# Retention over the prompt in chunks of 128, stacked sample rows in w_out, two expert slots loaded early, refills without a limit

## The chip, the cores and the metric

The kernel runs on one core of a Trainium2 chip, in one launch, in fp32 (some matmul operands are split into a high and a low part). The metric is the device time of one execution in microseconds. Engines: PE = TensorE, DVE = VectorE, ACT = ScalarE, POOL = GpSimd, SP = SyncE, which only issues DMAs here.

## What is computed

One inference step of one decoder layer for a prompt of 512 tokens and for 8 samples of 4 tokens each (32 rows), model width 1024. The token mixer has four retention heads (128 wide) and eight block-sparse attention heads (64 wide), a gated merge and an output projection; a layer norm, a mixture of 32 experts (two chosen per token within one of four groups) and a second layer norm follow. The retention of the prompt, as the reference has it:

```python
def retention_chunk(state, q, k, v):            # q, k, v of one chunk, L = 128
    log_g = jnp.log(retention_gammas())         # gamma_h = 1 - 2 ** (-5 - h)
    idx = jnp.arange(L, dtype=F32)
    diff = idx[:, None] - idx[None, :]
    decay = jnp.where(diff >= 0, jnp.exp(log_g[:, None, None] * jnp.maximum(diff, 0.0)), 0.0)
    inner = jnp.einsum('bhij,bhjv->bhiv', jnp.einsum('bhid,bhjd->bhij', q, k) * decay, v)
    q_dec = q * jnp.exp(log_g[:, None] * (idx + 1.0))[:, :, None]
    cross = jnp.einsum('bhid,bhdv->bhiv', q_dec, state)
    k_dec = k * jnp.exp(log_g[:, None] * (L - 1.0 - idx))[:, :, None]
    new_state = state * jnp.exp(log_g * L)[:, None, None] + jnp.einsum('bhjd,bhjv->bhdv', k_dec, v)
    return new_state, inner + cross
...
y = einsum(merged, w_out);  x = layer_norm(ALPHA * x + y)
hid = silu(einsum(t, w_eg)) * einsum(t, w_eu);  out = einsum(hid * combine, w_ed)
```

The state after the prompt is an output as well. The scan over chunks gives the same function as one product over all 512 positions with the decay between any two of them.

## The kernel before

The work runs in stages, one after the other on TensorE: 52 input projections with split operands; attention and retention; gates and branch projections; w_out with the first layer norm and the router; the routing; 16 pairs of experts; the gathering of the experts' rows and the second layer norm.

**Attention and retention.** The order of the work is written out by hand in the list `ORDER`. Each job has a kind: `S` is a score product into one of four PSUM banks in turn, `R` a VectorE step (`inv`: reciprocals and scaling of probabilities), `T` a turn (transpose) into two further banks, `O` a product into banks 6 and 7 in turn. TensorE may not write a product's bank until VectorE or ScalarE has emptied the product two before it (`s_ou`). Retention head h has score jobs `("ret", h, kb)`, kb = 0 to 3, that take the keys of one block of 128 against all queries from there on (512, 384, 256 and 128 columns). VectorE multiplies each by a table of decays (`decay`, 2048 columns of the constants) into `sd`, which holds one head. The job `reto` sums the ten blocks with the values; `rets` adds the four blocks' keys times values in one bank for the state, which VectorE copies to `rst` and SP stores (`store_head`). `mask_samples` is GpSimd's work for the samples' retention.

**w_out.** Five tiles of rows, t = 0 to 3 with 128 rows and t = 4 with the 32 rows of the samples. A tile has two halves of 512 columns, each half eight depth steps, each step three products: high rows by high weights, high rows by low weights, low rows by high weights. VectorE makes the low rows (`merged_low`), adds the result to ALPHA * x (`s_yu`), and does the layer norm. TensorE turns the normed rows, ScalarE copies them to `x1T` (two buffers) and TensorE runs the router on them (`router`).

**Experts.** An expert's weights are one row of 3072 columns a partition (1.57 MB): gate and up, 2048 columns, and down, 1024 columns, two DMAs. There are 11 slots for 32 experts: 0 to 7 in the arena, 8 in the memory of the constants, 9 in `scratch`, 10 in the projections' ring of weights. SP loads slots 0 to 2 and 10 during w_out, 3 to 7 when w_out's products are done, and 8 and 9 when routing has ended, as constants and routing's temporaries lie there till then. Then it refills slots: the gate and up part of pair n's slots when pair n's gate_up is done (`s_gu`, which starts at 1), the down part behind `s_dn`, with each load held until the load of two experts before it has landed:

```python
            QUEUED = 2

            def landed(sems, e):
                sp.wait_ge(sems[e % SLOTS], 16 * (e // SLOTS + 1))
```

GpSimd gathers a pair's token rows by indirect DMA from a copy of the normed rows in memory (`x1_d`, stored row tile by row tile in w_out), and scatters the experts' results likewise (`token_rows`). A pair's result rows have two buffers: VectorE, which writes them, waits for the scatter of two pairs before.

Of the kernel before, what the change touches and what calls it, by code (L numbers as in the profile page):

```python
# [34 lines left out]
P = 128  # L35
# [31 lines left out]
_CW = [("ident", P), ("before", P), ("ones", P), ("iota", P), ("dist", 512),  # L67
       ("decay", RH * 512), ("kdec", RH * 4), ("sdecay", RH * NS), ("qdec_s", RH * NS), ("kdec_s", RH),
       ("bcol", SB * NS), ("brow", SB), ("headmask", 4 * MH), ("sbias", NS + PAST + NS), ("own", MH),
       ("fold", 4 * SL),  # L70
       ("i4", NG), ("i8", EPG), ("e64", NE), ("tokid", 2 * TT), ("valid", TT), ("iv", OVT), ("eps", 1)]
CO = {}
# [7 lines left out]
def constants():  # L80
# [16 lines left out]
    m = np.arange(512)[None, :] - p[:, None]  # L97
    put("decay", P, np.stack([np.where(m >= 0, ks * np.exp(g * np.maximum(m, 0)), 0) for g in lg], 1))
    put("kdec", P, np.stack([ks * np.exp(g * (NP - 1 - (np.arange(4)[None, :] * P + p[:, None]))) for g in lg], 1))
# [47 lines left out]
def hybrid_step(nc, xT_d, x_d, w_tiles, w_out_d, w_router, b_router, b_merge, gn_g, ln1_g, ln1_b, ln2_g, ln2_b,  # L147
# [3 lines left out]
    with ExitStack() as ctx:  # L151
# [82 lines left out]
        sd = scratch[:, 2560:3840]  # L234
# [21 lines left out]
        logs = scratch[:, 2048:2048 + TT * 36].rearrange("p (t n) -> p t n", t=TT)  # L256
        rtr = scratch[:, 2304:5120]
# [43 lines left out]
        s_rst = sem("head_state_stored")  # L301
# [13 lines left out]
        s_qs = sem("sample_queries_spread")  # L315
        s_qm = sem("sample_queries_masked")
# [95 lines left out]
        def ret(h):  # L412
            return [("S", ("ret", h, kb)) for kb in range(4)]

        def turned(p):
            return [("T", ("moba", p, u, kb)) for u in range(2) for kb in range(4)]

# [6 lines left out]
        def O(*jb):  # L424
            return [("O", jb)]
# [65 lines left out]
        def _(sp):  # L491
# [64 lines left out]
            def store_head(h):  # L556
                sp.wait_ge(s_ou, done("rets", h))
                sp.dma_start(rpv[h], rst[:, h % 2]).then_inc(s_rst, 16)
# [63 lines left out]
            load_parts(10, experts_d[10])  # L622
# [18 lines left out]
            QUEUED = 2  # L641

            def landed(sems, e):
                sp.wait_ge(sems[e % SLOTS], 16 * (e // SLOTS + 1))
# [40 lines left out]
            sp.wait_ge(s_rst, 64)  # L685
# [4 lines left out]
        def _(pe):  # L690
# [58 lines left out]
            def scores(jb):  # L749
# [59 lines left out]
            def products(jb):  # L809
# [11 lines left out]
                elif jb[0] == "reto":  # L821
                    h = jb[1]
                    pe.wait_ge(s_su, used(("ret", h, 3)))
                    for qb in range(4):
                        for kb in range(qb + 1):
                            o = KT_OFF[kb] + (qb - kb) * P
                            m = mm(ps[:, b, qb * P:(qb + 1) * P], sd[:, o:o + P], rv_t[:, kb, h * P:(h + 1) * P],
                                   start=kb == 0, stop=kb == qb)
                elif jb[0] == "rets":
                    h = jb[1]  # L830
                    pe.wait_ge(s_kdec, 1)
                    for kb in range(4):
                        m = mm(ps[:, b, 0:P], rk_t[:, kb, h * P:(h + 1) * P], rv_t[:, kb, h * P:(h + 1) * P],
                               start=kb == 0, stop=kb == 3)
# [98 lines left out]
            def router(t):  # L933
                r = P if t < 4 else NS
                pe.wait_ge(s_x1c, t + 1)
                for k in range(KD):
                    m = mm(ps[0:r, 6, t * 36:(t + 1) * 36], x1T[:, t % 2, k, 0:r], wr[:, k, :],
# [6 lines left out]
            for t in range(TT):  # L944
# [3 lines left out]
                for half in range(2):  # L948
                    out, cols = ps[0:r, 2 * (t % 2) + half, :], slice(half * 512, (half + 1) * 512)
                    for k in range(KD):  # L950
# [127 lines left out]
        def _(act):  # L1078
# [139 lines left out]
            for t in range(TT):  # L1218
# [5 lines left out]
                if t >= 2:  # L1224
                    act.wait_ge(s_lg, t - 1)
                for q in range(2):
                    m = A(x1T[:, t % 2, 4 * q:4 * q + 4, 0:r],
# [61 lines left out]
        def _(pool):  # L1289
# [52 lines left out]
            mask_samples(0)  # L1342
            pool.wait_ge(s_o, done("cross", 0))
# [53 lines left out]
        def _(dve):  # L1397
# [41 lines left out]
            def scores(jb):  # L1439
# [19 lines left out]
                elif jb[0] == "ret":  # L1459
                    _, h, kb = jb  # L1460
                    w = NP - kb * P
                    if h > 0:
                        dve.wait_ge(s_o, done("reto", h - 1))
# [445 lines left out]
```

## Time and profile before

| | us |
|---|---|
| median of 3 runs (698.0 to 707.33) | 698.1 |
| profiled execution | 700.69 |
| its span in the trace | 698.8 |
| mean granted clock of TensorE | 0.957 |

Stages in the span, by TensorE's lines: projections 0 to 197, attention 197 to 295, gates and branches 295 to 440, w_out 440 to 503.5, routing 503.5 to 538, experts 538 to 662, the end to 698.8. Times in the trace are microseconds from the span's start. A matmul's listed length runs over its successor's start, as they are pipelined: the distance between two starts is what it costs. The profile's waits are those of one execution, the one in the third line of the table.

### The profile page before, as it was taken

What the parts mean: (1) busy time and instruction counts of PE and PEld (TensorE: products, weight loads), DVE (VectorE), ACT (ScalarE), POOL (GpSimd) and SP (SyncE); (2) the same over time, 40 slices, a digit from 0 to 9 for tenths busy, and PEclk for the clock granted to TensorE, in tenths of its full rate; (3) what the DMA queues carried; (4) which work ended last, traced back from release to release, by engine and by line L of the source; (5) the groups of instructions that cost most, each with busy time, mean ns of one, the idle gap of its engine ahead of it and who ended that gap; (6) DMA issues with size and microseconds to landing.
All of it is one profiled execution on the core that took longest, in us unless ns stands there. A gap on an engine that the chain in (4) does not pass through costs nothing.

```text
span 698.8 us, 11114 instructions
## 1 busy us (share of the span) xinstructions
PE 628.8 (90%) x4445; PEld 516.0 (74%) x4445; DVE 305.3 (44%) x599; ACT 146.0 (21%) x300; POOL 70.7 (10%) x74
## 2 busy tenths in 40 slices
PE   3999999999989897799999999999932899998886
PEld 3999999999965574699999998788532555554431
DVE  6344343354247458624445455363465022121226
ACT  0111101031164425300011112210110322321222
POOL 0101400030040000000000000000002123330114
PEclk9999999999999999889999999999955899999997
DMA  9425322227216444113343312870087899999573
GB/s 352 161 74 172 114 65 85 77 74 230 90 50 197 125 129 152 53 48 86 117 151 121 121 31 91 308 301 31 31 313 265 340 397 415 395 373 385 203 278 128
DMA packets 45978, 124.53 MB, mean 178 GB/s; under 512 B 6290, under 2 KB 19730, under 8 KB 41715
## 3 DMA queue, kind: packets, MB, share of 16 engines
q1 hardware_dynamic: 39888, 112.33, 45.5%
q0 software_dynamic: 4752, 8.93, 3.5%
q10 hardware_dynamic: 1298, 2.73, 1.0%
q8 instruction: 27, 0.44, 0.3%
q14 instruction: 13, 0.10, 0.0%
HBM read 114.72 MB, written 17.43 MB: 189 GB/s over the span
## 4 chain that ended last, share of the span: by engine, by line
PE 69%; DMA 18%; DVE 8%; ACT 2%; issue 2%; SPq 0%; POOLq 0%; DVEq 0%
PE ps L701 13%; PE ps L699 13%; PE ps L700 13%; DMA arena<-experts 10%; PE ps L694 3%; DMA scratch<-experts 3%; PE ps L961 3%; PE ps L963 3%; PE ps L962 3%; PE ps L1073 3%; PE ps L913 2%; PE ps L915 2%; PE ps L914 2%; DMA cst<-experts 1%; DMA w_ring<-experts 1%
## 5 line engine op out<-in xcount | busy, mean ns | idle before, releaser
L699 PE MATMUL ps<-xa_hi,w_hi 128*128 128x272 f32 x704 | 207.2, 294 | 10.5 <-DVE xa_lo L1418 10.5
L701 PE MATMUL ps<-xa_hi,w_lo 128*128 128x272 f32 x704 | 205.7, 292 | 0.0
L700 PE MATMUL ps<-xa_lo,w_hi 128*128 128x272 f32 x704 | 205.0, 291 | 0.0
L699 PEld LDWEIGHTS ps<-xa_hi,w_hi 128*128 128x128 f32 x704 | 135.0, 192 | 11.9 <-issue 9.8
L700 PEld LDWEIGHTS ps<-xa_lo,w_hi 128*128 128x128 f32 x704 | 135.2, 192 | 0.0
L701 PEld LDWEIGHTS ps<-xa_hi,w_lo 128*128 128x128 f32 x704 | 134.8, 192 | 0.0
L1409 DVE CAST w_hi<-w_ring 128x1024 fp32r<-128x1024 f32 x52 | 38.0, 730 | 116.2 <-PE ps L701 87.1
L1411 DVE TENSOR_TENSOR w_lo<-w_ring,w_hi 128x1024 fp32r<-128x1024 f32 x52 | 65.7, 1263 | 1.8
L1004 PE MATMUL ps<-arena,work 128*64 128x256 f32 x384 | 50.7, 400 | 6.1 <-DMA arena<-experts 3.7
L1351 POOL DMA_INDIRECT work<-x_rows,idx_i x13 | 13.3, 1025 | 355.4 <-DVE idx_i L1764 326.3
L1004 PEld LDWEIGHTS ps<-arena,work 128*64 128x64 f32 x384 | 31.0, 144 | 20.7 <-issue 6.6
L1429 DVE COPY arena<-ps 128x512 f32 x20 | 13.8, 690 | 59.7 <-PE ps L694 59.7
L1099 ACT ACTIVATE scratch<-ps 128x544 f32<-128x544 f32 x20 | 12.5, 624 | 126.4 <-PE ps L701 126.4
L913 PE MATMUL ps<-o_parts,w_hi 128*128 128x272 f32 x128 | 36.9, 289 | 1.6 <-DVE scratch L1591 1.6
L915 PE MATMUL ps<-o_parts,w_lo 128*128 128x272 f32 x128 | 36.9, 288 | 0.0
L914 PE MATMUL ps<-o_parts,w_hi 128*128 128x272 f32 x128 | 36.9, 288 | 0.0
L1787 DVE COPY work<-ps 128x512 f32<-128x512 f32 x31 | 20.0, 686 | 36.6 <-PE ps L1019 36.6
L1178 ACT ACTIVATE scratch<-ps,bm 128x544 f32<-128x544 f32 x16 | 11.5, 716 | 114.2 <-PE ps L701 114.2
L694 PE MATMUL ps<-cst,scratch 128*128 128x128 f32 (+1 forms) x180 | 27.9, 281 | 6.0 <-ACT arena L1146 3.7
L1781 DVE TENSOR_TENSOR work<-work,ps 128x128 f32<-128x128 f32 x16 | 4.6, 288 | 63.8 <-ACT work L1251 63.8
L694 PEld LDWEIGHTS ps<-cst,work 128*128 128x128 f32 x120 | 14.0, 146 | 23.5 <-issue 23.5
L694 PEld LDWEIGHTS ps<-cst,scratch 128*128 128x128 f32 (+1 forms) x180 | 19.3, 136 | 13.1 <-ACT arena L1146 7.8
(238 smaller groups left out, 890.6 us busy)
## 6 DMA issues: line engine op xcount, KB each, us to landing
w_ring<-w_tiles SPq DMA_DIRECT2D x52, 512.0 KB, 3.5
arena<-experts SPq DMA_DIRECT2D x24, 1024.0 KB, 10.2
arena<-experts SPq DMA_DIRECT2D x24, 512.0 KB, 10.0
arena<-kT_pool SPq DMA_DIRECT2D x16, 256.0 KB, 3.2
out<-arena SPq DMA_DIRECT2D x4, 1024.0 KB, 5.9
arena<-v_pool SPq DMA_DIRECT2D x16, 256.0 KB, 3.0
arena<-token_rows SPq DMA_DIRECT2D x8, 512.0 KB, 7.1
cst<-experts SPq DMA_DIRECT2D x3, 1024.0 KB, 8.4
```

Of the source, the lines that this page charges most:

```text
L694: return nc.tensor.transpose(out, in_, ident[0:rows, 0:rows])
L699: mm(out, w_hi[b][:, w], x_hi[:, k_x, cols], start=start, stop=False)
L700: mm(out, w_hi[b][:, w], x_lo[:, k_x, cols], start=False, stop=False)
L701: return mm(out, w_lo[b][:, w], x_hi[:, k_x, cols], start=False, stop=stop)
L913: mm(out, w_hi[m % 2][:, w], o_r[:, hi + k, cols], start=k == 0, stop=False)
L914: mm(out, w_hi[m % 2][:, w], o_r[:, lo + k, cols], start=False, stop=False)
L915: x = mm(out, w_lo[m % 2][:, w], o_r[:, hi + k, cols], start=False, stop=k == 3)
L961: mm(out, hi, wo_part(k, 0)[:, cols], start=k == 0, stop=False)
L962: mm(out, hi, wo_part(k, 1)[:, cols], start=False, stop=False)
L1004: m = mm(ps[s * CAP:(s + 1) * CAP, 2 + u, 0:2 * P], xgT[:, u, k, s * CAP:(s + 1) * CAP], wgu(slots[s], k), start=k == 0, stop=k == KD - 1)
L1409: v.tensor_copy(w_hi[b][:], w_ring[:, j, :]).then_inc(s_hi, 1)
L1411: v.tensor_tensor(w_lo[b][:], w_ring[:, j, :], w_hi[b][:].bitcast(F32), ALU.subtract).then_inc(done, 1)
```

## The change

The scores of a retention head are taken within each chunk of 128 only, four products of 128 columns in one bank, and masked by one VectorE multiply with `cmask`. GpSimd multiplies the queries by their decay beforehand (`s_qd`). `rets` leaves its four products apart; VectorE makes the running states `past_st` of the first three chunks and the final one from them, and `reto` adds the decayed queries times the past state to the product within the chunk. `rets` stands directly behind `ret` in the order. In w_out's last tile, the low rows lie beside the high rows in one stationary operand, and VectorE adds both halves of the result's rows. Slots 8 and 9 are loaded behind slot 10; what lay in their memory is placed elsewhere, `x1T` with one buffer. Refills are no longer held for earlier loads.

```diff
-_CW = [("ident", P), ("before", P), ("ones", P), ("iota", P), ("dist", 512),
-       ("decay", RH * 512), ("kdec", RH * 4), ...
+_CW = [("ident", P), ("dist", 512),
+       ("cmask", RH * P), ("qdec", RH * P), ("room", RH * 2 * P), ("kdec", RH * 4), ...
...
-        x1T = scratch[:, 3072:5120].rearrange("p (u k t) -> p u k t", u=2, k=KD)
+        x1T = w_ring[:, 3, :].rearrange("p (k t) -> p k t", k=KD)
...
         def ret(h):
-            return [("S", ("ret", h, kb)) for kb in range(4)]
+            return [("S", ("ret", h))] + O("rets", h)
...
-                 + moba(1) + ret(0) + O("pv", 0) + O("rets", 0) + inv(1) + [("T", ("samp", 0))] + O("reto", 0)
-                 + ret(1) + O("sampv", 0) + O("rets", 1) + turned(1) + O("sel", 0) + O("reto", 1)
-                 + moba(2) + ret(2) + O("pv", 1) + [("S", ("samp", 1))] + O("rets", 2) + inv(2) + O("cross", 1)
-                 + O("reto", 2) + ret(3) + [("R", ("samp", 1))] + turned(2) + O("rets", 3) + skv(1) + O("reto", 3)
+                 + moba(1) + ret(0) + O("pv", 0) + inv(1) + [("T", ("samp", 0))] + O("reto", 0)
+                 + ret(1) + O("sampv", 0) + turned(1) + O("sel", 0) + O("reto", 1)
+                 + moba(2) + ret(2) + O("pv", 1) + [("S", ("samp", 1))] + inv(2) + O("cross", 1)
+                 + O("reto", 2) + ret(3) + [("R", ("samp", 1))] + turned(2) + skv(1) + O("reto", 3)
...
-            load_parts(10, experts_d[10])
+            for s in (10, 8, 9):
+                load_parts(s, experts_d[s])
...
-            sp.wait_ge(s_nov, 1)
-            sp.wait_ge(s_idx, 1)
-            for s in (0, 1):
-                load_parts(8 + s, experts_d[8 + s])
...
                 for e in next_experts(n):
-                    landed(s_ed, e - QUEUED)
                     sp.dma_start(expert(e % SLOTS)[:, GU:EW], experts_d[e][:, GU:EW]).then_inc(s_ed[e % SLOTS], 16)
...
                 for e in next_experts(n):
-                    landed(s_e, e - QUEUED)
                     sp.dma_start(expert(e % SLOTS)[:, 0:GU], experts_d[e][:, 0:GU]).then_inc(s_e[e % SLOTS], 16)
...
-                    _, h, kb = jb
-                    m = mm(ps[:, b, 0:NP - kb * P], fm[:, 4 * FM_OF[RK] + h, kb * P:(kb + 1) * P],
-                           fm[:, 4 * FM_OF[RQ] + h, kb * P:NP], start=True, stop=True)
+                    h = jb[1]
+                    pe.wait_ge(s_qd, 1)
+                    for c in range(4):
+                        cols = slice(c * P, (c + 1) * P)
+                        m = mm(ps[:, b, cols], fm[:, 4 * FM_OF[RK] + h, cols], fm[:, 4 * FM_OF[RQ] + h, cols],
+                               start=True, stop=True)
...
-                    pe.wait_ge(s_su, used(("ret", h, 3)))
-                    for qb in range(4):
-                        for kb in range(qb + 1):
-                            o = KT_OFF[kb] + (qb - kb) * P
-                            m = mm(ps[:, b, qb * P:(qb + 1) * P], sd[:, o:o + P], rv_t[:, kb, h * P:(h + 1) * P],
-                                   start=kb == 0, stop=kb == qb)
+                    pe.wait_ge(s_su, used(("ret", h)))
+                    pe.wait_ge(s_ou, done("rets", h))
+                    for c in range(4):
+                        cols = slice(c * P, (c + 1) * P)
+                        m = mm(ps[:, b, cols], sd[:, h % 2, cols], rv_t[:, c, h * P:(h + 1) * P], start=True, stop=c == 0)
+                        if c > 0:
+                            m = mm(ps[:, b, cols], fm[:, 4 * FM_OF[RQ] + h, cols], past_st[:, h % 2, c - 1, :],
+                                   start=False, stop=True)
...
+                        if t == TT - 1:
+                            hi_lo = m_hi[:, t % 2, k, 0:2 * NS]
+                            mm(out, hi_lo, wo_part(k, 0)[:, cols], start=k == 0, stop=False)
+                            m = mm(out, hi_lo, wo_part(k, 1)[:, cols], start=False, stop=k == KD - 1)
+                            continue
...
-                if t >= 2:
-                    act.wait_ge(s_lg, t - 1)
+                act.wait_ge(s_lg, t)
...
             mask_samples(0)
+            for h in range(RH):
+                q = fm[:, 4 * FM_OF[RQ] + h, 0:NP].rearrange("p (c n) -> p c n", c=4)
+                m = pv.tensor_tensor(q, q, C("qdec").rearrange("p (h n) -> p h n", h=RH)[:, h:h + 1, :]
+                                     .to_broadcast([P, 4, P]), ALU.mult)
+            m.then_inc(s_qd, 1)
...
-                    m = v.tensor_copy(rst[:, h % 2], ps[:, bank, 0:P])
+                    state = past_st[:, h % 2]
+                    ch.link(v.tensor_copy(state[:, 0], ps[:, bank, 0:P]))
+                    for c in range(1, 4):
+                        m = v.scalar_tensor_tensor(state[:, c] if c < 3 else rst[:, h % 2], state[:, c - 1],
+                                                   float(GAMMAS[h] ** P), ps[:, bank, c * P:(c + 1) * P],
+                                                   ALU.mult, ALU.add)
+                        if c < 3:
+                            ch.link(m)
...
+                if t == TT - 1:
+                    ch.link(m)
+                    for q in range(2):
+                        m = v.tensor_tensor(z[:, q * 512:(q + 1) * 512], z[:, q * 512:(q + 1) * 512],
+                                            ps[NS:2 * NS, 2 * (t % 2) + q, :], ALU.add)
```

## Rows read from the trace of the kernel before

**Rows 1.** Page, chain that ended last: shares of the span by engine.

```profile
PE 69%; DMA 18%; DVE 8%; ACT 2%; issue 2%; SPq 0%; POOLq 0%; DVEq 0%
```

**Rows 2.** Windows: PE, PEld, DVE, ACT, POOL busy us (count), granted clock, DMA, GB/s.

```profile
472.00:476.00 4.00, 4.00 (x19) 3.25 (x19) 0.00 (x0) 0.00 (x0) 0.00 (x0) 1.00 0.00 0
...
552.00:556.00 4.00, 4.00 (x38) 2.62 (x34) 0.29 (x1) 0.28 (x1) 0.00 (x0) 1.00 0.84 289
...
560.00:564.00 4.00, 4.00 (x32) 2.21 (x30) 0.29 (x1) 1.36 (x3) 1.44 (x2) 1.00 1.02 381
...
648.00:652.00 4.00, 3.46 (x21) 1.48 (x17) 1.04 (x3) 1.64 (x4) 0.00 (x0) 1.00 0.95 326
```

**Rows 3.** Chain in order of time, 530 to 700: start, us, what.

```profile
538.79 13.15 DMA scratch<-experts
...
552.33 5.41 DMA arena<-experts
...
663.68 3.17 DMA token_rows<-work,row_i
```

**Rows 4.** Timeline, TensorE, experts: start, us, engine, line, operation, tiles, shapes, count.

```profile
549.06 1.21 PE L694 MATMUL ps<-cst,work 128*128 128x128 f32 x9
551.33 3.67 PE L1004 MATMUL ps<-arena,work 128*64 128x256 f32 x32 [1.06 <-ACT work L1246]
...
558.09 3.67 PE L1004 MATMUL ps<-arena,work 128*64 128x256 f32 x32
...
653.03 0.40 PE L1004 MATMUL ps<-cst,work 128*64 128x256 f32 x1 [1.57 <-DMA scratch<-experts]
```

**Rows 5.** Timeline, TensorE, 214 to 223 us, retention's first head.

```profile
214.14 2.42 PE L765 MATMUL ps<-arena 128*128 128x512 f32 x8
216.49 2.38 PE L819 MATMUL ps<-arena 128*64 128x512 f32 x16
218.79 1.16 PE L833 MATMUL ps<-arena 128*128 128x128 f32 x8
219.79 0.49 PE L694 MATMUL ps<-cst,lg_s 128*128 128x128 f32 x3
220.36 2.50 PE L827 MATMUL ps<-arena,scratch 128*128 128x128 f32 x20
222.69 1.02 PE L765 MATMUL ps<-arena 128*128 128x512 f32 x2
```

**Rows 6.** Timeline, VectorE, 223 and 260 us.

```profile
223.21 0.69 DVE L1496 COPY arena<-ps 128x512 f32<-128x512 f32 x1
223.81 0.88 DVE L1498 BATCH_NORM_STATS2 gstat<-ps 128x6 f32<-128x128 f32 x4
...
260.61 2.48 DVE L1470 SCALAR_TENSOR_TENSOR arena<-arena,ps 128x512 f32<-128x512 f32 x4 [0.70 <-PE ps L785]
```

**Rows 7.** Timeline, GpSimd and VectorE, 202 to 209 us.

```profile
202.02 1.04 POOL L1336 TENSOR_TENSOR w_ring<-arena,cst 128x512 f32<-128x512 f32 x1
...
205.63 1.27 DVE L1481 TENSOR_SCALAR scratch<-scratch,small 128x128 f32<-128x128 f32 x4
...
207.02 1.88 DVE L1481 TENSOR_SCALAR scratch<-scratch,small 128x128 f32<-128x128 f32 x4
```

**Rows 8.** Timeline, TensorE and VectorE, end of w_out.

```profile
499.65 0.39 PE L962 MATMUL ps<-w_out_early,merged_hi 128*32 128x512 f32 x1
499.88 0.40 PE L963 MATMUL ps<-w_out_early,merged_lo 128*32 128x512 f32 x1
...
503.76 1.27 DVE L1637 SCALAR_TENSOR_TENSOR arena<-arena,ps 32x512 f32<-32x512 f32 x2 [7.95 <-PE ps L963]
```

**Rows 9.** DMA, 548 to 655: issues, count, median us from issue to landing.

```profile
token_rows<-work,row_i POOLq DMA_INDIRECT x14, 8.1
```

**Rows 10.** DMA queues, 564.4 to 567.6: packets, MB, share of 16 engines.

```profile
q1 hardware_dynamic: 205, 0.97, 75.5%
q0 software_dynamic: 141, 0.26, 21.3%
```

More of the change, by code:

```diff
@@ L64 @@
 FM_OF = {MK: 0, RK: 1, MQ: 2, RQ: 3}
-_CW = [("ident", P), ("before", P), ("ones", P), ("iota", P), ("dist", 512),
-       ("decay", RH * 512), ("kdec", RH * 4), ("sdecay", RH * NS), ("qdec_s", RH * NS), ("kdec_s", RH),
+_CW = [("ident", P), ("dist", 512),
+       ("cmask", RH * P), ("qdec", RH * P), ("room", RH * 2 * P), ("kdec", RH * 4), ("sdecay", RH * NS), ("qdec_s", RH * NS), ("kdec_s", RH),
        ("bcol", SB * NS), ("brow", SB), ("headmask", 4 * MH), ("sbias", NS + PAST + NS), ("own", MH),
        ("fold", 4 * SL),
-       ("i4", NG), ("i8", EPG), ("e64", NE), ("tokid", 2 * TT), ("valid", TT), ("iv", OVT), ("eps", 1)]
+       ("before", P), ("ones", P), ("iota", P), ("i4", NG), ("i8", EPG), ("e64", NE), ("tokid", 2 * TT), ("valid", TT), ("iv", OVT), ("eps", 1)]
 CO = {}
@@ L96, in constants @@
     ks = float(P) ** -0.5
-    m = np.arange(512)[None, :] - p[:, None]
-    put("decay", P, np.stack([np.where(m >= 0, ks * np.exp(g * np.maximum(m, 0)), 0) for g in lg], 1))
-    put("kdec", P, np.stack([ks * np.exp(g * (NP - 1 - (np.arange(4)[None, :] * P + p[:, None]))) for g in lg], 1))
+    put("cmask", P, np.stack([np.where(p[None, :] >= p[:, None], ks * np.exp(-g * (p[:, None] + 1)), 0) for g in lg], 1))
+    put("qdec", P, np.tile(np.stack([np.exp(g * (p + 1)) for g in lg], 0)[None], (P, 1, 1)))
+    put("kdec", P, np.tile(np.stack([ks * np.exp(g * (P - 1 - p)) for g in lg], 1)[:, :, None], (1, 1, 4)))
     j = np.arange(NS)
@@ L252, in hybrid_step @@
         t_b = scratch[:, 2176:2720]
-        x1T = scratch[:, 3072:5120].rearrange("p (u k t) -> p u k t", u=2, k=KD)
+        x1T = w_ring[:, 3, :].rearrange("p (k t) -> p k t", k=KD)
         ln_g = scratch[:, 0:1024]
         ln_b = scratch[:, 1024:2048]
-        logs = scratch[:, 2048:2048 + TT * 36].rearrange("p (t n) -> p t n", t=TT)
-        rtr = scratch[:, 2304:5120]
+        rtr = work[:, 4096:6400]
+        logs = work[:, 6700:6700 + TT * 36].rearrange("p (t n) -> p t n", t=TT)
         oh_lo = work[:, 0:2 * TT * P].rearrange("p (n q) -> p n q", n=2 * TT)
@@ L300, in hybrid_step @@
         s_idle = sem("idle_written")
-        s_rst = sem("head_state_stored")
+        s_rst = [sem(f"head_state_stored{u}") for u in range(2)]
         s_st = sem("states_loaded")
@@ L315, in hybrid_step @@
         s_qs = sem("sample_queries_spread")
+        s_qd = sem("retention_queries_decayed")
         s_qm = sem("sample_queries_masked")
@@ L684, in _ @@
             sp.wait_ge(s_x1s, 16 * TT)
-            sp.wait_ge(s_rst, 64)
+            for u in range(2):
+                sp.wait_ge(s_rst[u], 32)
             sp.wait_ge(s_out, 16 * (2 + TT))
@@ L831, in products @@
                     pe.wait_ge(s_kdec, 1)
-                    for kb in range(4):
-                        m = mm(ps[:, b, 0:P], rk_t[:, kb, h * P:(h + 1) * P], rv_t[:, kb, h * P:(h + 1) * P],
-                               start=kb == 0, stop=kb == 3)
+                    for c in range(4):
+                        m = mm(ps[:, b, c * P:(c + 1) * P], rk_t[:, c, h * P:(h + 1) * P], rv_t[:, c, h * P:(h + 1) * P],
+                               start=True, stop=True)
                 elif jb[0] == "cross":
@@ L936, in router @@
                 for k in range(KD):
-                    m = mm(ps[0:r, 6, t * 36:(t + 1) * 36], x1T[:, t % 2, k, 0:r], wr[:, k, :],
+                    m = mm(ps[0:r, 6, t * 36:(t + 1) * 36], x1T[:, k, 0:r], wr[:, k, :],
                            start=k == 0, stop=k == KD - 1)
@@ L948, in _ @@
                 for half in range(2):
-                    out, cols = ps[0:r, 2 * (t % 2) + half, :], slice(half * 512, (half + 1) * 512)
+                    out, cols = ps[0:r if t < 4 else 2 * NS, 2 * (t % 2) + half, :], slice(half * 512, (half + 1) * 512)
                     for k in range(KD):
@@ L1459, in scores @@
                 elif jb[0] == "ret":
[L1460 to L1463, printed above, removed]
-                    m = v.tensor_tensor(sd[:, KT_OFF[kb]:KT_OFF[kb] + w], ps[:, bank, 0:w],
-                                        C("decay").rearrange("p (h n) -> p h n", h=RH)[:, h, 0:w], ALU.mult)
+                    h = jb[1]
+                    if h >= 2:
+                        dve.wait_ge(s_o, done("reto", h - 2))
+                    m = v.tensor_tensor(sd[:, h % 2].rearrange("p (c n) -> p c n", c=4),
+                                        ps[:, bank, :].rearrange("p (c n) -> p c n", c=4),
+                                        C("cmask").rearrange("p (h n) -> p h n", h=RH)[:, h:h + 1, :]
+                                        .to_broadcast([P, 4, P]), ALU.mult)
                 else:
@@ L1501, in products @@
                     if h >= 2:
-                        dve.wait_ge(s_rst, 16 * (h - 1))
-                    m = v.tensor_copy(rst[:, h % 2], ps[:, bank, 0:P])
+                        dve.wait_ge(s_rst[h % 2], 16)
+                        dve.wait_ge(s_o, done("reto", h - 2))
+                    state = past_st[:, h % 2]
[6 more added lines that the diff above has]
+                            ch.link(m)
                 elif jb[0] == "cross":
@@ L1601, in merged_low @@
                 dve.wait_ge(s_mh, n)
-                v.tensor_tensor(m_lo[:, k0:k1, cols], merged[:, k0:k1, cols],
+                low = m_lo[:, k0:k1, cols] if t < 4 else m_hi[:, t % 2, :, NS:2 * NS]
+                v.tensor_tensor(low, merged[:, k0:k1, cols],
                                 m_hi[:, t % 2, k0:k1, 0:P if t < 4 else NS].bitcast(F32), ALU.subtract).then_inc(s_ml, 1)
```

16 lines of the change are left out of this document (7 added, 9 removed).

## The prediction

> **What bounds the kernel now.** I began with the chain of work that ended last [rows 1]: TensorE holds 69% of the span and DMA 18%, so the question for each part is in which of the two regimes it lies. Windows of 4 us give the border. From the start to about 503 us TensorE is the chain; between 448 and 503 the DMA engines lie idle for whole windows (472 to 476) while TensorE is full [rows 2]. In the experts' stage, 538 to 662, the DMA share is near 1 in the windows from 552 to 652, as at 560 (1.02, 381 GB/s); three lie visibly below it, 552 (.84), 648 (.95) and, like the last, 628 [rows 2]. There the chain runs load to load: it begins with the slot loads at 538.79, hands over to a refill issued at 552.33, and ends with the load on which pair 15's first matmul waits, at 653.03 [rows 3, 4]. TensorE could go faster: with its weights there, a pair takes 558.09 − 551.33 = 6.76 us [rows 4]. So the change touches three stages: two bound by TensorE (attention, w_out), one by DMA (experts).
>
> **Retention in chunks.** A gap between two starts on TensorE is what one step costs the chain. Old scores: 216.49 − 214.14 = 2.35. Old `rets`, four products of 128 columns: 219.79 − 218.79 = 1.00. Old `reto`, ten products: 222.69 − 220.36 = 2.33 [rows 5]. The new scores are again four products of 128 columns, so 1.00, saving 1.35. The new `reto` has 4 + 3 products, 7/10 × 2.33 = 1.63, saving .70. `rets` keeps its four. Sum 2.05 a head, 8.2 us for four, if nothing else is late.
>
> Three things are late. First, products share two PSUM banks in turn, and `rets` moves ahead of `pv` and `inv`. The second job behind `reto(0)`, which takes its bank, was `rets(1)` and is now `sampv(0)`. VectorE empties `reto(0)` only after its `inv(1)` work, with a copy of .69 and statistics of .88 that ended at 224.7 [rows 6]; faster products bring that end forward by .4 at most, since `inv(1)` and not TensorE decides it. On TensorE `sampv(0)` would come at 222.69 − 1.35 − .70 + 1.00 + 1.00 = 222.6, in front of a bank that is free at 224.3: a wait of 1.7 us, which leaves 2.4 of 4.1 us for the first two heads. Second, at the last head VectorE is in four masked additions of 2.48 us from 260.61 before it empties `reto(3)` [rows 6]; the .7 us saved there is hidden behind them, and 3.4 of 4.1 are left for the last two heads. Third, GpSimd gets four multiplies of 128x512, 1.04 each by its row at 202.02, run from about 203 to 207.3, beside VectorE's scalings. Four of those took 1.27 us with GpSimd idle and 1.88 beside its work [rows 7], so .6 for each four that are overlapped, and the second four already were. GpSimd's next masking, and with it that overlap, moves to behind 207.3. I charge 1.0 (between 0 and 2). `s_qd` rises near 208 and the first score product that waits for it comes at 214.14, so the wait is covered by 6 us; without the cover the whole 4.2 us would stand on TensorE, with moba(1)'s turns queued behind. `mask_samples(1)`, the only thing queued behind the multiplies, is wanted some 30 us later.
>
> On the side of VectorE four multiplies become one (.69 by the copy of that size), while `rets` becomes a copy and three chained additions of 128x128: there is no row for such a chain, so between .9 (three at the .29 that a 128x128 copy costs) and 2 us; I take 1.0, about what the multiplies give back, and `reto` comes several jobs later. Storing the head's state is a DMA that nobody on the chain waits for. Net: 2.4 + 3.4 − 1.0 = 4.8 us, with bounds of 2 (banks and VectorE take most) and 8.2.
>
> The Trainium skill ("SBUF — State Buffer", section "SBUF: two separate sides") says that GpSimd and VectorE share a port pair as an exclusive lock, held for a whole instruction, and that the loser blocks. By it each VectorE operation with two SBUF inputs could wait one whole multiply of 1.04, up to 4.2 us in all; the rows show .6 for four operations, which is less than one lock each, and my 1.0 goes by the rows. With 4.2 in its place attention would give 1.6 and the median would be 689.9, between the forecast and the third rival.
>
> **The stacked sample rows.** At tile t = 4 of w_out the products start .23 us apart (499.65 to 499.88) though each is listed with .39 [rows 8]. 48 become 32: 16 × .23 = 3.7 us less. The stationary operand is 64 columns wide in place of 32; the moving side is 512 either way, and in the window from 472 products of 128 stationary columns run at the same pitch (19 in 4 us, those cut by its edges counted [rows 2]), so the width costs 0. VectorE pays: two more additions of 32x512, which cost 1.27 as the pair in 503.76 does [rows 8], behind a link between dependent instructions (within .1). This stands in a row of dependent steps that lead to the routing, so −3.7 + 1.3 = −2.4. What could hide it is the router's wait on the same rows, and that only moves with them. The low part moves from one tile to another at the same cost.
>
> **Slots 8 and 9 early.** 3.15 MB at 381 GB/s are 8.3 us of DMA, moved from 538 to about 448. They push the first store of `x1` rows back (it waits in the same queue), which nothing reads before the gathers behind the routing, and end before the idle window at 472 [rows 2]. SP issues four more DMAs ahead of its waits for `x1` rows and has nothing else to do there. The constants that had to outlive slot 8 and `x1T`, `logs`, `rtr` only change place. `x1T` has one buffer in place of two: ScalarE's copy of tile t waits for the router of t − 1, which TensorE runs ahead of the turn that the copy needs anyway: 0; if that order were different, one router pass per tile (about 1 us) would stand there.
>
> The gain: with slots 8 and 9 in place, the first refill no longer waits for slot 9's landing. It was issued at 552.33 [rows 3], and pair 0's gate_up, on which it then waits alone, ended at 549.06 [rows 4]. All refills are one full queue from there to 653, so the head start of 3.2 us carries to its end.
>
> **No limit on refills.** What a deeper queue can fill are the windows with a share below full: 4 × (.16 + .05 + .05) = 1.0 us. Together 4.2 us. The lower bound is 0 (DMA is full already and the order alone changes), the upper comes from TensorE: pair 15 can't start sooner than 551.33 + 14 × 6.76 = 645.97, against 653.03: 7.1.
>
> Sum: 4.8 + 2.4 + 4.2 = 11.4 us. The profiled execution took 700.69 (span 698.8) and the median of the runs is 698.1; I take the difference off the median: 698.1 − 11.4 = 686.7 (profiled 689.3).
>
> **Rivals.** *The gathers and scatters drown (slower side).* Gathers and scatters of token rows go by another queue to the same engines. A scatter landed 8.1 us after its issue (median of 14) beside a full queue [rows 9], and 3.17 us in the chain with the queue empty [rows 3]. If that latency is the backlog ahead of it, lifting the limit lets it grow: a pair frees 3.15 MB each 6.76 us, in which DMA moves 6.76 × .381 = 2.58 MB, .54 of it the pair's gather and scatter (7.13 MB of the software queue over 13 pairs); the backlog grows by 1.1 MB or 2.9 us a pair. Results are double buffered: pair n's rows wait for the scatter of n − 2, two pairs or 13.5 us, of which I estimate 2.9 to be used up by two copies of .69 and the issue. From 3.2 on, latency passes 10.6 us with the third refill, and the pairs feel it from about the sixth. From there they come at the DMA's pace, 3.69 MB / .381 = 9.7 us: pairs 6 to 12 from 585.1 to 643.3, three more at 6.76 give pair 15 at 663.6, 10.5 later than now. 698.1 − 4.8 − 2.4 + 10.5 = 701.4. Against it: in 564.4 to 567.6, soon after a scatter's issue, the software queue moved 141 packets beside the loads' 205 [rows 10]; they alternate, the small ones don't wait until the loads are done.
>
> The Trainium skill ("DMA: Bandwidth & Descriptors", section "Queues, rings and completion order") has both: engines go round between queues at packet granularity, which is against this rival, and a semaphore's increment lands only after the earlier writes of that engine, across queues, which is for it. By the first the time is the forecast's, by the second up to this rival's. The packets above agree with the first; no run here shows the second for a deeper backlog.
>
> *DMA is full and stays so.* The earlier refills only take from each other, and the stage ends as before: 698.1 − 7.2 = 690.9. For it: a share of 1.0 over nearly the whole stage; against it: the share at 552 is .84, and 3.15 MB really leave the stage.
>
> *Retention gives nothing.* The two banks, VectorE and GpSimd take all of it: 698.1 − 2.4 − 4.2 = 691.5.
>
> **How the numbers follow.** Forecast as worked out .53, drowning .17, DMA full .15, retention nothing .12, others .03. The likeliest gives 686.7. Its own range: 681 (attention at 8.2 and experts at 7.1 would be 680.4) to 692 (attention at 2 and half of the experts' 4.2 would be 691.6). For 8 in 10 the range runs from 680, both upper ends met, to 698, which holds both 691 rivals with their own bounds; the drowned case, above it, stays out. 2% is about what a measurement here can tell from no change, so 684.1 and 712.1 are the bounds: faster holds the better half of the forecast's cases, less what lies within 2.6 us of 686.7: .25; slower needs a drowning twice as dear as worked out: .03; the same .72.
>
> **What would show it.** Retention: four score products of 128 columns and seven outputs a head, an idle time of about 1.7 us on TensorE ahead of `sampv(0)`, and scalings near 205 at 1.3 to 1.9 for four. w_out: 32 products in the last tile, two new additions of about 1.27. Experts: the first refill issued as pair 0's gate_up ends, pair 15 at about 4 us sooner relative to routing's end, scatters still landing in 8 to 10 us. Drowning would show as scatters of 15 us and more, and as TensorE waiting for VectorE in pairs 6 to 12. Wrong are the numbers if TensorE's granted clock falls in a stage where it now is full, if the DMA rate changes with a deep queue, or if TensorE reaches the DMA's place sooner and the gain is the 7.1 of its own pace.

## The result, and the profile after

The changed kernel took 694.29 us in the median of 8 runs (692.35 to 696.56), the kernel before 700.04 in 8 runs of the same comparison: ratio 0.9922, 95% interval 0.9899 to 0.9946. One of those eight runs took 1184.4 us; it and the other slow runs are left out of every ratio, not out of the medians. The changed kernel is faster, by 5.5 us (3.8 to 7.1): the interval is clear of 1, the gain is under the 2% of the forecast's bounds and about half of the 11.4 forecast. The profiled execution took 694.20 (span 692.4, mean granted clock 0.951), against 700.69 (698.8, 0.957).

TensorE's timeline of the changed kernel, first retention head and experts:

```profile
217.32 1.16 PE L761 MATMUL ps<-arena 128*128 128x128 f32 x8
218.31 1.06 PE L831 MATMUL ps<-arena 128*128 128x128 f32 x8
219.30 2.37 PE L815 MATMUL ps<-arena 128*64 128x512 f32 x16
...
221.99 0.61 PE L823 MATMUL ps<-arena,scratch 128*128 128x128 f32 x4
...
223.55 1.06 PE L761 MATMUL ps<-arena 128*128 128x128 f32 x8
...
227.36 1.92 PE L852 MATMUL ps<-arena 128*32 128x512 f32 x16 [1.86 <-DVE gstat L1506]
...
544.17 1.21 PE L687 MATMUL ps<-cst,work 128*128 128x128 f32 x9
...
643.68 0.40 PE L1007 MATMUL ps<-cst,work 128*64 128x256 f32 x1 [2.12 <-DMA scratch<-experts]
```

Beside [rows 5]: scores 218.31 − 217.32 = .99 in place of 2.35, `reto` 223.55 − 221.99 = 1.56 in place of 2.33, and the wait ahead of `sampv(0)` that the forecast placed there, 1.86. Beside [rows 4]: from the end of pair 0's gate_up (544.17) to pair 15 (643.68) are 99.5 us, before they were 653.03 − 549.06 = 104.0.

VectorE, then GpSimd, in the same execution:

```profile
204.69 3.62 DVE L1489 TENSOR_SCALAR scratch<-scratch,small 128x128 f32<-128x128 f32 x4
...
208.43 2.26 DVE L1489 TENSOR_SCALAR scratch<-scratch,small 128x128 f32<-128x128 f32 x4
...
497.09 1.27 DVE L1654 SCALAR_TENSOR_TENSOR arena<-arena,ps 32x512 f32<-32x512 f32 x2 [4.29 <-PE ps L961]
498.40 1.28 DVE L1659 TENSOR_TENSOR arena<-arena,ps 32x512 f32<-32x512 f32 x2
```

```profile
202.08 4.96 POOL L1347 TENSOR_TENSOR arena<-arena,cst 128x512 f32<-128x512 f32 x4
207.00 2.04 POOL L1335 TENSOR_TENSOR w_ring<-scratch,cst 128x128 f32<-128x128 f32 x4
```

The two sets of four scalings of `inv(0)` (128, 256, 384 and 512 columns wide; a row names the first) took 3.62 and 2.26 us, against 1.27 and 1.88 [rows 7]. The multiplies run from 202.08 to 207.04. Two of the four had ended when the scalings began; the other two lie beside the first two scalings, one each:

```profile
204.56 1.26 POOL L1347 TENSOR_TENSOR arena<-arena,cst 128x512 f32<-128x512 f32 x1
205.78 1.26 POOL L1347 TENSOR_TENSOR arena<-arena,cst 128x512 f32<-128x512 f32 x1
```

```profile
204.69 1.21 DVE L1489 TENSOR_SCALAR scratch<-scratch,small 128x128 f32<-128x128 f32 x1
...
205.82 1.37 DVE L1489 TENSOR_SCALAR scratch<-scratch,small 128x256 f32<-128x256 f32 x1
```

Each of these two ended about .1 us behind the multiply beside it. TensorE, which turns the scaled rows, waited for them, and behind the wait its granted clock fell. First the trace before, then the changed kernel (the windows' columns as in [rows 2]):

```profile
206.96 0.99 PE L694 MATMUL ps<-cst,scratch 128*128 128x128 f32 x7 [0.74 <-DVE scratch L1481]
```

```profile
208.00:212.00 4.00, 3.14 (x21) 1.94 (x21) 3.55 (x8) 2.72 (x8) 1.80 (x3) 1.00 0.81 226
```

```profile
208.37 2.81 PE L687 MATMUL ps<-cst,scratch 128*128 128x128 f32 x10 [3.08 <-DVE scratch L1489]
211.33 2.81 PE L687 MATMUL ps<-cst,scratch 128*128 128x128 f32 x10 [0.16 <-ACT arena L1149]
```

```profile
208.00:212.00 4.00, 3.43 (x13) 2.50 (x14) 3.96 (x9) 1.68 (x4) 2.08 (x4) 0.51 0.83 234
212.00:216.00 4.00, 3.95 (x21) 2.67 (x20) 2.16 (x10) 2.36 (x7) 0.00 (x0) 0.63 0.78 246
```

The wait grew from .74 to 3.08 us, and the turns behind it ran at the lower of the clock's two levels, 1.2 in place of 2.4 GHz.

In w_out the gap to [rows 8] is 503.76 − 497.09 = 6.7 us at the first addition and 5.4 behind the two new ones (1.31); what the stages ahead of w_out gained is in it.

SP's queue and the DMAs from 548 to 655 (median us from issue to landing last):

```profile
544.28 6.68 SPq L648 DMA_DIRECT2D arena<-experts  x4
...
609.59 6.42 SPq L648 DMA_DIRECT2D cst<-experts  x1
```

```profile
arena<-experts SPq DMA_DIRECT2D x14, 1024.0 KB, 22.9
...
token_rows<-work,row_i POOLq DMA_INDIRECT x15, 8.0
```

The first refill goes out .1 us behind the end of gate_up 0. The loads in the first row now land 22.9 us after their issue (median of 14), so the queue is deep, and yet a scatter lands in 8.0, as before [rows 9].

The chain that ended last, in order of time, and four windows (columns as in [rows 2]):

```profile
619.85 23.70 DMA scratch<-experts
643.55 0.14 issue
643.68 5.36 PE ps L1007 x32
...
656.02 3.16 DMA token_rows<-work,row_i
...
664.58 15.67 PE ps L1076 x32
```

```profile
640.00:644.00 4.00, 1.89 (x13) 0.59 (x9) 1.29 (x2) 0.84 (x3) 0.58 (x1) 1.00 0.56 226
644.00:648.00 4.00, 4.00 (x27) 2.89 (x25) 0.00 (x0) 0.00 (x0) 0.39 (x1) 0.63 0.28 112
...
660.00:664.00 4.00, 2.51 (x6) 0.76 (x4) 0.00 (x0) 0.00 (x0) 0.00 (x0) 1.00 0.88 308
664.00:668.00 4.00, 3.42 (x5) 1.50 (x6) 0.00 (x0) 0.00 (x0) 0.00 (x0) 0.69 1.02 408
```

Here too the granted clock falls in two windows, each behind one in which TensorE waited. There gate_up of pair 15 took 5.36 us, 3.67 in the execution before, and the 32 products of the final combine 15.67 in place of 13.97: 3.4 us together.

Where the 6.4 us between the two spans lie, from equal places in both traces: attention (first to fourth group of block-sparse scores, 66.3 against 67.4) −1.1, with the low clock at 208 in it; w_out −2.3; the start of gate_up 0 to pair 15 −4.0 (4.5 from its end, as gate_up 0 itself took .5 longer); pair 15 itself +1.7; the end +1.2. Another −2.0 lie in stretches with the same instructions in both, −.95 at 16 us and −1.06 at 300, where the granted clock rose earlier; these I don't count as the change's.

### The profile page after: what moved, and what is told of

It reads as the page before. It is cut to its first block, busy times and chain, and to the rows that moved or that the text cites. A ratio compares the mean times of both kernels' runs of the same rounds, so it can differ in the third digit from the quotient of the medians.

```text
span 692.4 us, 11013 instructions
## 1 busy us (share of the span) xinstructions
PE 619.0 (89%) x4405; PEld 510.2 (74%) x4405; DVE 308.7 (45%) x601; ACT 146.3 (21%) x300; POOL 75.4 (11%) x78
## 4 chain that ended last, share of the span: by engine, by line
PE 78%; DVE 9%; DMA 6%; ACT 3%; issue 2%; SPq 2%; POOLq 0%; DVEq 0%; ACTq 0%
PE ps L694 13%; PE ps L692 13%; PE ps L693 13%; PE ps L1007 6%; PE ps L687 6%; DMA scratch<-experts 3%; PE ps L1022 3%; PE ps L1076 3%; PE ps L911 2%; PE ps L964 2%; PE ps L913 2%; PE ps L912 2%; PE ps L966 2%; PE ps L965 2%; PE ps L754 1%
## 5 line engine op out<-in xcount | busy, mean ns | idle before, releaser
L687 PE MATMUL ps<-cst,scratch 128*128 128x128 f32 (+1 forms) x180 | 30.0, 297 | 7.6 <-DVE scratch L1489 3.8
L687 PEld LDWEIGHTS ps<-cst,scratch 128*128 128x128 f32 (+1 forms) x180 | 20.7, 144 | 16.1 <-ACT arena L1149 7.7
```

Source lines behind the costliest of these rows:

```text
L687: return nc.tensor.transpose(out, in_, ident[0:rows, 0:rows])
```

## The experiments

All ratios are to the kernel before, run on the same chip. The groups e1 to e4, e5 to e8, e9 to e12, and e13 with e14 each ran on a chip of their own, so times of different groups are compared by their ratios. The last two columns come from one profiled execution of each kernel. "Attention" is the distance from the first block-sparse scores to the second start of the last pair's; "experts" that from the end of gate_up 0 to pair 15.

| run | median us | ratio (95%) | attention us | experts us |
|---|---|---|---|---|
| before | 700.04 | 1 | 67.4 | 104.0 |
| after | 694.29 | 0.9922 (.9899 to .9946) | 66.3 | 99.5 |
| e1 chunks only | 700.11 | 0.9994 (.9963 to 1.0024) | 66.3 | 103.1 |
| e2 stacked only | 697.55 | 0.9979 (.9945 to 1.0013) | 67.4 | 102.2 |
| e3 early slots only | 700.50 | 0.9990 (.9959 to 1.002) | 67.4 | 101.4 |
| e4 no limit only | 697.86 | 0.9965 (.9936 to .9994) | 67.4 | 100.3 |
| e5 no multiply | 690.03 | 0.9835 (.9795 to .9875) | 62.2 | 99.3 |
| e6 multiply later | 690.84 | 0.9857 (.9816 to .9897) | 62.2 | 99.4 |
| e7 states behind | 692.91 | 0.9884 (.9843 to .9925) | 65.2 | 99.7 |
| e8 limit back | 694.10 | 0.9904 (.9865 to .9944) | 66.4 | 100.2 |
| e9 filled waits | 697.43 | 0.9957 (.9934 to .9979) | 66.7 | 101.8 |
| e10 both mended | 687.23 | 0.9824 (.9791 to .9857) | 60.3 | 99.5 |
| e11 both and filled | 690.61 | 0.9875 (.9841 to .9909) | 60.9 | 101.2 |
| e12 chunks held | 695.85 | 0.9938 (.9914 to .9962) | 62.2 | 102.1 |
| e13 shorter fill | 693.88 | 0.9918 (.9888 to .9948) | 67.1 | 99.5 |
| e14 mended, shorter fill | 687.57 | 0.9814 (.9779 to .9848) | 60.3 | 99.4 |

**One part at a time.** The kernel before with the lines of one part of the change.

```diff
 # e1: all lines of the change on ret, rets, reto, sd, past_st, cmask, qdec, s_qd, s_rst and ORDER
+            return [("S", ("ret", h))] + O("rets", h)
```

> The kernel before with the retention in chunks alone. By the forecast's step attention gains 4.8 us and the median falls by that, 0.7%. By the theory formed from the trace after (GpSimd's four multiplies hold VectorE's two sets of four scalings for about 2.7 us and the turns behind them for 3.8), attention gains only about 1.1, so a ratio of 0.998, and the first four scalings of inv(0) take about 3.6 us as they do after, not 1.3.

Measured: 0.9994, attention 66.3. VectorE's timeline of this kernel:

```profile
205.55 3.62 DVE L1495 TENSOR_SCALAR scratch<-scratch,small 128x128 f32<-128x128 f32 x4
...
209.29 2.26 DVE L1495 TENSOR_SCALAR scratch<-scratch,small 128x128 f32<-128x128 f32 x4
```

The forecast's 4.8 us are outside the interval (a gain of at most 2.6 us); the scalings are as long as after.

```diff
 # e2
+                        if t == TT - 1:
+                            hi_lo = m_hi[:, t % 2, k, 0:2 * NS]
...
+                            continue
```

> The kernel before with the stacked sample rows alone. Both theories: w_out ends 3.7 us sooner on TensorE, two additions of 1.29 give 1.3 back, 2.4 us off the median, ratio 0.9966. If the stage behind hides it, ratio 1.000.

Measured: 0.9979, 1.5 us with an interval that holds both 2.4 and 0. Its trace has the two new additions at 1.28 and the routing's rows behind them.

```diff
 # e3, with x1T, rtr, logs and the constants placed as in the change
+            for s in (10, 8, 9):
...
-            for s in (0, 1):
-                load_parts(8 + s, experts_d[8 + s])
```

> The kernel before with slots 8 and 9 early and nothing else; the limit of two experts stays. By the forecast's split the first refill starts at the end of pair 0's gate_up, 3.2 us sooner, and the stage ends 3.2 us sooner, ratio 0.9954. If the depth of the queue is what counts, the limit holds the refills back again and less than 1.5 us is left.

```diff
 # e4
-                    landed(s_ed, e - QUEUED)
...
-                    landed(s_e, e - QUEUED)
```

> The kernel before with the limit on refills taken away and nothing else. By the forecast's split 1.0 us. If instead the limit keeps the DMA engines short all through the stage (372 to 387 GB/s in many windows of before against 410 to 425 after), it is worth 3 us or more by itself, since slot 9's landing then no longer holds the first refill either.

Measured: 0.9990 for the early slots, 0.9965 for the limit. SP's queue in e3, then in e4, where gate_up 0 ended at 549.60 and 548.31:

```profile
549.72 9.79 SPq L653 DMA_DIRECT2D arena<-experts  x4
```

```profile
548.42 6.67 SPq L654 DMA_DIRECT2D arena<-experts  x4
```

In both the first refill goes out as gate_up 0 ends: the held refill was freed by either edit, and the forecast's 3.2 us can't be given to the early slots alone. What is more, in e1 and e2, which have the old loads, slot 9 landed sooner and the refill went out within .9 us of gate_up 0's end (548.43 against 547.79 in e1). The 3.2 us were partly that one profiled execution. Against the mean of the four executions with the old loads (before, e1, e2, e12: 102.8) the stage is 1.4 us shorter with the early slots, 2.5 without the limit, and 3.4 with both (99.5, the mean of the executions with both and no filling, 99.3 to 99.7). These differences rest on one execution each for the single edits.

**The multiplies.** The changed kernel without them (e5 leaves out the queries' decay, so its retention has other values), and with them held back.

```diff
 # e5
-            for h in range(RH):
-                q = fm[:, 4 * FM_OF[RQ] + h, 0:NP].rearrange("p (c n) -> p c n", c=4)
-                m = pv.tensor_tensor(q, q, ...)
-            m.then_inc(s_qd, 1)
+            pool.sem_inc(s_qd, 1)
```

> The changed kernel without GpSimd's four multiplies (the queries' decay is left out, which changes the retention's values). If they cost VectorE and the turns 3.8 us, the time falls to about 690.5 (ratio to before 0.987) and the first four scalings of inv(0) take 1.3 us again. By the forecast's charge of 1.0 it falls by 1 us only.

```diff
 # e6
             mask_samples(0)
+            pool.wait_ge(s_pn, 8)
             for h in range(RH):
```

> The changed kernel with the same four multiplies held until the eight scalings of inv(0) are done (GpSimd waits for s_pn at 8). If it is the overlap with operations that have both ends in SBUF that costs, the gain is that of the run without the multiplies, about 4 us, since they then lie beside operations that read PSUM. If GpSimd slows VectorE whatever it does, or the late s_qd holds the first score product, 1 us or less is gained.

Measured: 0.9835 and 0.9857, attention 62.2 in both. VectorE's timeline of e5:

```profile
205.29 1.27 DVE L1485 TENSOR_SCALAR scratch<-scratch,small 128x128 f32<-128x128 f32 x4
...
206.68 1.88 DVE L1485 TENSOR_SCALAR scratch<-scratch,small 128x128 f32<-128x128 f32 x4
```

VectorE and GpSimd in e6:

```profile
204.69 1.27 DVE L1490 TENSOR_SCALAR scratch<-scratch,small 128x128 f32<-128x128 f32 x4
...
206.08 1.27 DVE L1490 TENSOR_SCALAR scratch<-scratch,small 128x128 f32<-128x128 f32 x4
...
207.28 2.47 DVE L1479 SCALAR_TENSOR_TENSOR arena<-arena,ps 128x512 f32<-128x512 f32 x4
```

```profile
207.44 4.97 POOL L1348 TENSOR_TENSOR arena<-arena,cst 128x512 f32<-128x512 f32 x4 [5.32 <-DVE scratch L1490]
```

This is the experiment that decides: the same four multiplies, 5.4 us later, cost nothing. Beside them lie now additions that read PSUM and SBUF, and they take 2.47 us as they did before the change with little of GpSimd's work beside them. What the multiplies stretch are the scalings, which have both ends in SBUF.

TensorE in e6, and its granted clock:

```profile
206.02 0.98 PE L687 MATMUL ps<-cst,scratch 128*128 128x128 f32 x7 [0.74 <-DVE scratch L1490]
...
213.20 1.16 PE L761 MATMUL ps<-arena 128*128 128x128 f32 x8
```

```profile
208.00:212.00 4.00, 3.39 (x24) 2.32 (x24) 2.95 (x11) 2.71 (x11) 4.00 (x4) 1.00 0.74 224
```

The work ahead of the turns starts at 204.14 in both traces, so the 4.1 us can be split. The turns start 208.37 − 206.02 = 2.35 later in the changed kernel: that is VectorE. From there to the first retention scores it takes 217.32 − 208.37 = 8.95 us, and 213.20 − 206.02 = 7.18 in e6: the other 1.8 lie in the stretch at the lower clock. The clock falls at this place in all six profiled executions with the multiplies beside the scalings (after, e1, e7, e8, e9, e13) and in none of the ten others. At full clock TensorE might have waited for VectorE's second set instead, so 1.8 is the most that the clock by itself took there.

```diff
 # e12: e1 with the wait of e6
+            pool.wait_ge(s_pn, 8)
```

> The kernel before with the retention in chunks alone, and the multiplies held until inv(0) is done. If the overlap is what ate the retention's gain, attention takes 62.2 us in place of 67.4 and the median falls by some 5 us, ratio 0.993; if the gain is lost later for another reason (w_out, the DMA stage), attention is short and the median falls by less than 2.5.

Measured: 0.9938, so 4.3 us, attention 62.2. The retention's gain does reach the end of the kernel when the multiplies are out of the way; e1, without the wait, gained .4.

**The bank.**

```diff
 # e7
-                 + ret(1) + O("sampv", 0) + turned(1) + O("sel", 0) + O("reto", 1)
+                 + ret(1)[0:1] + O("sampv", 0) + O("rets", 1) + turned(1) + O("sel", 0) + O("reto", 1)
```

> The changed kernel with the state products of head 1 put behind sampv(0), as before. If the 1.86 us that TensorE waits ahead of sampv(0) are the two product banks, the wait goes and 1.5 to 1.9 us of the median with it; if VectorE's order is what ends the stretch, the wait moves to the next product and nothing is gained.

Measured: 692.91, attention 1.2 us shorter than after. TensorE's timeline has no wait there:

```profile
224.39 1.92 PE L852 MATMUL ps<-arena 128*32 128x512 f32 x16
226.24 1.12 PE L854 MATMUL ps<-arena 32*128 32x512 f32 x2
227.29 1.16 PE L831 MATMUL ps<-arena 128*128 128x128 f32 x8
```

The wait was the bank's. The difference to the changed kernel, 1.4 us by the medians and 2.7 by the ratios, lies within the intervals.

```diff
 # e10: e6 and e7 together
```

> The changed kernel with the multiplies held until inv(0) is done and head 1's state products behind sampv(0). If the two costs are separate, attention from the first moba score to moba(3)'s second start takes 66.3 - 4.1 - 1.2 = 61.0 us and the median falls by some 5 us against the changed kernel. If they are one wait seen twice, it is that of the multiplies held alone, 62.2.

Measured: 687.23, ratio 0.9824, attention 60.3 (61.0 expected). The two costs are separate; this version beats both kernels.

**The limit.**

```diff
 # e8: the changed kernel
+                    landed(s_ed, e - QUEUED)
...
+                    landed(s_e, e - QUEUED)
```

> The changed kernel with the limit of two experts put back. By the forecast's split it loses 1.0 us. If the deep queue is what keeps the DMA engines at 415 GB/s, it loses 2.5 us or more; if the deep queue does nothing, it is the same.

Measured: 0.9904, experts 100.2 against 99.5. With slots 8 and 9 early, the limit costs .6 us in the stage and nothing that the median tells.

**The clock.** Products on the identity in TensorE's two last waits.

```diff
 # e9
+                for _ in range(16 if n == PAIRS - 1 else 0):
+                    mm(ps[:, 2 + u, 3 * P:4 * P], ident, ident, start=True, stop=True)
                 gate_up(pair_slots(n), u, ...)
...
             for t in range(4):
+                for _ in range(16 if t == 3 else 0):
+                    mm(ps[:, 7, 0:P], ident, ident, start=True, stop=True)
                 own_rows(t)
```

> The changed kernel with 16 products of 128 columns on the identity put into TensorE's wait ahead of pair 15 and 16 more ahead of the last tile's own rows in the final combine, in PSUM that nobody reads. If it is the idle time ahead of the two stretches that lets the granted clock fall, pair 15's gate_up takes 3.7 us and not 5.4, the 32 products of the combine 14.0 and not 15.7, and the median falls by 2 to 3.4 us. If the clock falls for another reason, both stay long and the time is that of the changed kernel.

Measured: 697.43, by the ratios 2.5 us slower than the changed kernel, just more than the two intervals together leave open. TensorE's timeline:

```profile
643.87 3.74 PE L1033 MATMUL ps<-cst 128*128 128x128 f32 x32
...
668.09 13.90 PE L1080 MATMUL ps<-arena,work 128*128 128x512 f32 x32
```

The combine is at full speed, and gate_up 15 (in the chain at 647.61) took 3.60; but the filling is 3.6 us where the waits were 2.1, some 3.0 more in the two places together.

```diff
 # e11: e10 with the filling of e9
```

> The run before with the filled waits as well. If idle time sets the clock in the two stretches, another 2 to 3.4 us of the median, and a smaller spread between its runs; if not, the same as the run before.

Measured: 690.61, 3.4 us slower than e10, about the same 3.0. That the longer filling is the reason in both is worked out from its length; no run measures it apart.

```diff
 # e13 (e14: e10 with the same)
+                for _ in range(8 if n == PAIRS - 1 else 0):
...
+                for _ in range(8 if t == 3 else 0):
```

> The changed kernel with half the filling: 8 products ahead of pair 15 and 8 ahead of the last tile's own rows, 1.8 us each, less than the 2.1 us that TensorE waits in each place. The longer filling kept the granted clock at 1.00 in both stretches, but at 3.6 us it outlasted the waits. If idle time sets the clock there, this one gives gate_up at 3.7 and the combine at 14.0 and 2 to 3 us off the changed kernel's median; if the clock needs more than the wait can hold, both stay long or the time doesn't move.

> Multiplies held, head 1's states behind sampv(0), and the shorter filling. Of the run with both mended the profile showed the full clock in both stretches already, but its slowest runs were 4 us longer than its fastest; if idle time makes that spread, this one's runs lie within 2 us, at about 686; if not, it is the same as without the filling or up to 2 us slower.

Measured: 693.88 and 687.57, as the same kernels without the filling. TensorE's timeline of e13:

```profile
643.27 1.95 PE L1033 MATMUL ps<-cst 128*128 128x128 f32 x16
645.56 0.40 PE L1007 MATMUL ps<-cst,work 128*64 128x256 f32 x1 [0.34 <-DMA scratch<-experts]
...
664.53 13.97 PE L1080 MATMUL ps<-arena,work 128*128 128x512 f32 x32
```

All four filled executions have the full clock in both stretches. But so have e5, e6 and e10 without any filling, and TensorE waited 2.1 us ahead of pair 15 in them too; so the filling isn't shown to be what holds the clock, nor a wait of 2.1 us to be enough to lower it. The medians did not move: e13's is .4 below the changed kernel's, within the intervals, and e14's six runs spread over 3.4 us as e10's over 4.3. In e13 a low clock shows elsewhere in attention (a group of scores of 3.12 us at 240, 2.05 in the trace after). How much of the 3.4 us that the profiled execution lost belongs to the change in the median stays open.

## Why the prediction was wrong

**Retention: the step that failed.** The products on TensorE were right to within .1 us each, and so were the bank in front of `sampv(0)` (1.7 forecast, 1.86 measured) and the hidden last .7 (the last group of block-sparse scores, first start to second, took 2.24 us before and 2.91 after). What failed is "I charge 1.0 (between 0 and 2)" for GpSimd's multiplies. Attention is 66.3 us with them as placed and 62.2 without or with them held: 4.1 us. Without them the change gives 5.2 of the 5.8 that the other two steps left. The term was wrong twice.

First, I had read [rows 7] as .6 for each four scalings beside any of GpSimd's work. But the 1.88 us stood beside instructions of 128x128, half a microsecond each; the multiplies are of 128x512, and the two scalings beside them took 1.21 and 1.37 us, against .29 and .35 in e6. That made TensorE's turns 2.35 us late. Second, the term priced VectorE alone. The longer wait on TensorE was followed by the lower clock, up to 1.8 us more. The prediction names that as a sign of being wrong ("if TensorE's granted clock falls in a stage where it now is full") and gives it no term; it came true here, in attention.

The Trainium skill ("SBUF — State Buffer", section "SBUF: two separate sides") has the rule that I set aside: an exclusive lock for a whole instruction. The trace agrees with it against my reading: the scaling's length went with that of GpSimd's instruction (1.21 and 1.37 beside 1.26, .55 to .67 beside masks of about .5), and operations on PSUM were spared (2.47). Not every overlapped scaling was held: one of 128 columns at 208.43, beside a mask, took .29. That the 4.2 us worked out from the rule are close to the 4.1 measured is chance: 4.2 stood for four multiplies, only two lay beside scalings, and up to 1.8 of the 4.1 are the clock's.

The rival "retention gives nothing" (691.5, given .12) had the right part and, with VectorE and GpSimd, the right place; it was the nearest of the rivals by mechanism.

**Stacked rows: right.** 3.7 us of products went, 1.31 came. In the trace 2.3 net; e2 alone can't tell 2.4 from 1.5.

**Early slots and the limit: the sum fits, the split does not.** 4.2 forecast; 4.5 between the two traces that I had, 3.4 between the means over all executions. By ratios, .9922 / (.9994 × .9979) = .9949, 3.6 us for both, with an uncertainty as large (the three 95% intervals together). But each edit alone starts the refills at gate_up 0's end, so 3.2 and 1.0 are not the two parts, and the 3.2 was one execution's slow landing.

**The clock: not in the sum.** The prediction named it only as what would make it wrong. In attention it went with the multiplies, six executions to none. Late in the profiled execution another 1.7 us were lost twice; other executions with waits of 1.7 to 2.1 us in the same places kept the clock, and what decides there stays open.

**Drowning: refuted.** The loads' backlog grew to 22.9 us, and the scatters stayed at 8.0. TensorE kept a pace of 6.75 us a pair until the loads ran out.

In all, of the 5.9 us between forecast and ratio 3.1 are the multiplies with the clock behind them, .6 attention's other steps and .6 the loads; the 1.6 that are left are less than what the clock took late in the profiled execution, and no more than these intervals leave open. What they are is not shown.

## What to carry to other kernels

Work moved to an idle GpSimd was free here beside VectorE operations that read PSUM, and dear beside scalings within SBUF; look up what VectorE does in that window, and price each overlapped operation with both ends in SBUF at up to one whole GpSimd instruction. Then ask which engine waits for it: here TensorE did, and its clock fell behind the wait. Here one wait on GpSimd, 5 us later, was worth nearly as much as the whole change. When two edits remove the same wait, take the gain once, and don't take a wait's length from one execution.

## What was not expected of the hardware

The multiplies took 4.97 / 4 = 1.24 us each with either kind of VectorE work beside them, where the prediction had 1.04 from the one masking row of 128x512; the new ones read a broadcast factor, and no run tells whether that is the reason. SP's own issue of a load, four in 6.68 us at the start, took 6.42 us for one once some 23 us of loads were queued. It looks as if the queue limits itself, which would be why taking the software's limit away changed so little; no run tests that. And a backlog of loads in one queue left the latency of another queue on the same engines as it was, 8.0 against 8.1 us.
